# Layer 0's attention in a different order of pairs: the prompt's blocks first, the memory pairs last, and the sample rows' steps up to two pairs earlier

## What is computed

```python
# prompt: causal, and of the keys it may see each query keeps the 128 with the best indexer score
vals, idx = lax.top_k(indexer_scores(iq, ik, iw, qpos, kpos), n_sel)
o = gqa_sparse_attend(q, take(kv, idx), isfinite(vals))     # 12 heads, 4 key/value heads
# memory: every prompt query against 256 memory tokens
p = softmax(einsum('bthd,bmhd->bhtm', mq, mem_k) * scale);  om = einsum('bhtm,bmhd->bthd', p, mem_v)
# sample: each of the 8 tokens against 256 of its 1024 cached keys and itself (paged cache), and its own 256 memory tokens
```

## Time and profile before

| | |
|---|---|
| median of 3 runs | 2230.3 us (2225.42 to 2233.84) |
| the profiled execution | 2222.14 us |
| its span, first to last instruction | 2220.2 us |
| PE busy in the span | 2103.8 us (95%) |
| DVE busy | 1015.3 us (46%) |
| ACT busy | 701.6 us (32%) |
| PE's mean granted clock | 0.973 of full speed |
| layer 0's attention, first scores to PE's turning of the sample rows' outputs | 585.35 to 731.79 us |
| layer 1's attention, first scores to last output | 1676.63 to 1788.4 us |

### The profile page before, as it was taken

One profiled execution on the slowest core, in us unless ns is written; L12 is line 12 of the kernel. 1 busy time (PEld: TensorE's weight loads), 2 busy tenths in 40 slices (PEclk: granted clock), 3 DMA queues, 4 the chain that ended last, 5 costly groups with the idle time before them and its releaser, 6 DMA issues.

```text
span 2220.2 us, 43049 instructions
## 1 busy us (share of the span) xinstructions
PE 2103.8 (95%) x17509; PEld 2003.5 (90%) x17509; DVE 1015.3 (46%) x1463; ACT 701.6 (32%) x869; POOL 336.8 (15%) x301
## 2 busy tenths in 40 slices
PE   6999999989868899999999999999997789999997
PEld 6999999968635899999999999999995579999997
DVE  7433333566895443333354333335533353333334
ACT  5332222431235333322243322224124443321232
POOL 2110011233222111001111100111511121100111
PEclk9999999989979999999999999999999989999998
DMA  6324423322552232332244234224236012223222
GB/s 222 121 91 141 154 92 106 108 64 65 193 167 76 85 138 83 139 124 94 73 140 152 94 109 147 90 98 173 87 110 231 8 60 93 90 86 109 80 74 74
DMA packets 60067, 246.57 MB, mean 111 GB/s; under 512 B 8642, under 2 KB 30538, under 8 KB 42930
## 3 DMA queue, kind: packets, MB, share of 16 engines
q1 hardware_dynamic: 58082, 212.31, 28.5%
q10 hardware_dynamic: 1872, 32.67, 4.0%
HBM read 234.67 MB, written 34.80 MB: 121 GB/s over the span
## 4 chain that ended last, share of the span: by engine, by line
PE 88%; DVE 6%; ACT 2%; issue 2%; SPq 1%; DMA 0%; ACTq 0%; POOL 0%; DVEq 0%; POOLq 0%
PE ps L556 81%; PE ps L768 1%; PE ps L787 1%; DVE tkw L1791 1%; PE ps L747 1%; DVE tk L1788 1%; ACT pbuf L1188 1%; PE ps L755 1%; ACT wh L1049 1%; DVE a_sc L1860 1%; PE ps L947 1%; SPq L397 0%; DVE wl L1329 0%; PE ps L987 0%; DVE pbuf L1555 0%
## 5 line engine op out<-in xcount | busy, mean ns | idle before, releaser
L556 PE MATMUL ps<-xh,wh 128*128 128x260 f32 x3296 | 666.2, 283 | 3.6 <-ACT wh L1049 2.0
L556 PE MATMUL ps<-xh,wl 128*128 128x260 f32 x3296 | 665.2, 283 | 0.0
L556 PE MATMUL ps<-xl,wh 128*128 128x260 f32 x3296 | 664.2, 283 | 0.0
L1329 DVE TENSOR_TENSOR wl<-raw,wh 128x2048 fp32r<-128x2048 f32 x181 | 420.9, 2325 | 321.3 <-ACT wh L1049 321.3
L556 PEld LDWEIGHTS ps<-xh,wh 128*128 128x128 f32 x3296 | 509.6, 189 | 4.1 <-DVE memv L1382 2.2
L556 PEld LDWEIGHTS ps<-xh,wl 128*128 128x128 f32 x3296 | 509.3, 189 | 0.0
L556 PEld LDWEIGHTS ps<-xl,wh 128*128 128x128 f32 x3296 | 507.9, 189 | 0.0
L1049 ACT ACTIVATE wh<-raw 128x2048 fp32r<-128x2048 f32 x181 | 344.9, 1906 | 348.0 <-PE ps L556 297.0
L556 PE MATMUL ps<-acth,wh 128*128 128x260 f32 x1600 | 324.1, 284 | 10.0 <-DVE actl L1878 7.6
L556 PE MATMUL ps<-actl,wh 128*128 128x260 f32 x1600 | 324.4, 284 | 0.0
L556 PE MATMUL ps<-acth,wl 128*128 128x260 f32 x1600 | 323.4, 284 | 0.0
(11 more groups left out here) (264 smaller groups left out, 1612.3 us busy)
## 6 DMA issues: line engine op xcount, KB each, us to landing
raw<-in_w_ffn_in SPq DMA_DIRECT2D x88, 1024.0 KB, 4.9
raw<-in_w_ffn_out SPq DMA_DIRECT2D x32, 768.0 KB, 4.3
raw<-in_w_ffn_out SPq DMA_DIRECT2D x32, 640.0 KB, 3.9
raw<-in_w_in_b SPq DMA_DIRECT2D x10, 1024.0 KB, 5.0
raw<-in_w_in_a SPq DMA_DIRECT2D x9, 1024.0 KB, 4.9
out_state<-in_state ACTq DMA_DIRECT2D x8, 1022.0 KB, 6.8
ring_w<-in_kpool SPq DMA_DIRECT2D x48, 128.0 KB, 2.4
raw<-in_w_mem SPq DMA_DIRECT2D x4, 1024.0 KB, 7.1
```

The source lines that it names most:

```text
L556: mm = pe.matmul(o, w(kt), moving, start=(kt == 0 and i == 0), stop=(kt == nk - 1 and i == 2))
L1329: dve.tensor_tensor(wl[:, n % 2, :], raw[:, n % 2, :], wh[:, n % 2, :].bitcast(F32), ALU.subtract)\
```

## The change

`pairs_a` now returns the 24 prompt pairs first and the 8 memory pairs behind them: block 0 is u 0 to 5, block 1 is 6 to 11, block 2 is 12 to 17, block 3 is 18 to 23, memory is 24 to 31. Pairs below u = 20 share one PSUM room for their scores whatever their width, pairs from 20 on use two. The sample rows' steps from "even" on move forward by one or two pairs on PE ("even" from k = 6 to 5, "odd" from 13 to 11, "turn" from 16 to 14, "turn_new" from 18 to 16) and by two pairs on ACT; on DVE the masking of those scores moves from k = 14 to 12, and the inversions stay at k = 18. `VALUES_AFTER`, the search's four steps in each k, the ring of buffers and SP's order stay as they are. Layer 1 keeps its order and its rooms.

```diff
 def pairs_a():

-    pairs = pairs_mem(6)
+    pairs = []
     for blk in range(NBLK):
         for tile in range(len(PAIRS_A)):
             pairs.append(dict(kind="a", blk=blk, tile=tile, cols=(blk + 1) * P, kv=2 * (tile // 3), out=tile))
-    return pairs
+    return pairs + pairs_mem(6)
...
+        ROWS_UNTIL = 20
         ATTEND_AHEAD = {"mem": 2, "a": 2, "b": 1}
...
-                one = q["cols"] <= 256
+                one = u < ROWS_UNTIL if u < len(pairs[0]) else q["cols"] <= 256
...
-        ROWS_AT = {0: "first", 3: "turn_mem", 6: "even", 13: "odd", 16: "turn", 18: "turn_new"}
+        ROWS_AT = {0: "first", 3: "turn_mem", 5: "even", 11: "odd", 14: "turn", 16: "turn_new"}
         VALUES_AFTER = {20: ("mem", 0), 21: ("mem", 1), 23: ("a", 0), 30: ("a", 1)}
-        FIRST_WIDE = next(q["u"] for q in pairs[0] if q["cols"] > 256 and q["u"] % 2)
+        FIRST_WIDE = ROWS_UNTIL + 1
...
-                elif k == 15:
+                elif k == 13:
                     act.wait_ge(rows_masked, 2)
...
-                elif k == 17:
+                elif k == 15:
                     act.wait_ge(rows_turned, 2)
...
-                elif k == 19:
+                elif k == 17:
                     act.wait_ge(rows_turned, 3)
...
-                elif k == 14:
+                elif k == 12:
                     dve.wait_ge(r_used, items_of("a", "key", 0)[-1]["r"] + 1)
```

## The result

The changed kernel takes 2240.48 us (median of 14 runs, 2232.25 to 2245.69), the kernel before 2233.51 in 14 runs beside it (2225.42 to 2236.24). The ratio is 1.0034, with a 95% interval of 1.0023 to 1.0045: by it 7.6 us slower (5 to 10), less than the 0.5% that was called telling. The forecast had been +8.3 us, within 0.5%.

What follows compares the result with a forecast made beforehand. DVE's search was taken to set the pace until 672, PE after; waits and late value loads moved output turning from 731.79 to 740.1, +8.3 us. Added to 2230.3, this gave 2238.6 us, range 2229 to 2247.

Steps and rivals of the forecast that it cites:

- "odd" begins behind the last key load: Layer 0's attention: moved two pairs earlier, "odd" must wait on PE for the last key load, landing at 638.3.
- pair 18 masked, pair 19's scores begin: End of DVE's search: six remaining search steps and `select` run first; pair 18 masked at 674.0, scores 19 waiting for it.
- first cached values end: PE finishes the weighing after pair 23 at 707.2, where it was 699.05.
- The last value items: SP's unchanged 25.27 us load chain after pair 23 ends at 732.5; PE waits some 11 us instead of 1.75.
- the wait of "odd" for its load: PE reaches "odd" at about 635.6, stands until 638.3; DVE then stands 2.8 us (bounds 1.4 and 5).
- the first term: Start of the attention: the first three maskings and linked work are narrower, gaining 1.9 us by the end of step 1.
- a late "even": "Even" late by a us or two costs nothing, swallowed by the wait at "odd".
- PE from 676.15 to 709.83: PE's work from pair 18 masked to first cached values' end: 31.5 us plus 1.7 for half clock.
- Half clock after the long wait: Last cached values, 4.16 us before, take 1.5 us more after 11 idle us (bounds 0 and 4).
- PE at half clock through block 2: Rival, steps 12 to 15: DVE waits 1.7 us in each; +15 us, 2245.5; chance 0.18.
- The hidden last loads: Rival: the last value loads cause no wait; -4.8 us, 2225.5; chance 0.08.
- a gain: Rival: over 11 us faster, needing DVE's stage to end earlier with more pairs masked; chance 0.02 for the rest.

Runs made afterwards that it cites:

- a_values_early: Changed kernel with the sample rows' values weighed after pairs 17, 18, 19, 30 instead of 20, 21, 23, 30; stretch 145.4 us, ratio 0.9982 to the kernel before.
- b_rows_early: Kernel before, its pair order kept, with only the sample rows' steps moved forward as in the change; stretch 147.9 us, ratio 0.9989 to the kernel before.
- a_numbers_ahead: Changed kernel with SP reading the last three sequences' page numbers earlier, while waiting for a buffer; stretch 149.5 us, ratio 1.0003 to the kernel before.
- mem_between_only: Changed kernel with memory pairs moved between blocks 2 and 3, values and four-step search unchanged; stretch 145.2 us, ratio 1.0004 to the kernel before.
- mem_between: Changed kernel with memory pairs between blocks 2 and 3, values after 17, 18, 19, 30, search spread to k = 19; stretch 132.8 us, ratio 0.9930 to before.
- mem_between_late: Same as mem_between, but values weighed after pairs 20, 21, 23, 30 as in the changed kernel; stretch 147.4 us, ratio 1.0003 to the kernel before.
- a_search_five: Changed kernel with five search steps in each k instead of four; stretch 154.7 us, ratio 1.0035 to the kernel before.
- a_rows_later: Changed kernel with the sample rows' steps from "even" on one k later (6, 12, 15, 17); stretch 156.0 us, ratio 1.0020 to the kernel before.
- b_values_early: Same as b_rows_early, but values weighed after pairs 17, 18, 19, 30; stretch 141.3 us, ratio 0.9993 to the kernel before.

## Why the prediction was right, point by point

With 2.1 us added for the later start of the stretch, the forecast's times stand against the rows above as follows:

| step of the prediction | forecast + 2.1 | measured |
|---|---|---|
| "odd" begins behind the last key load | 640.4 | 640.64 |
| "odd" ends | 645.4 | 645.49 |
| pair 14 masked from | 647.8 | 647.84 |
| pair 18 masked, pair 19's scores begin | 676.1 | 676.15 |
| first cached values end | 709.3 | 709.83 |
| last values begin | 734.6 | 734.94 |
| last values end | 740.3 | 740.93 |
| outputs turned | 742.2 | 743.01 |

**The last value items** decided, as forecast: +8.3 in the sum, +9.1 in the stretch, +7.6 timed. That the values' place in the new order, not the sample rows' moved steps, did it is shown by a_values_early and b_rows_early; that 8.3 of the 25 us are register loads on SP, by a_numbers_ahead. (The prediction's "23 us up to the last landing" are the issuing alone; the last load landed some 2 us behind it.) On the Trainium skill's page "DMA: Bandwidth & Descriptors", section "Issuing engines are not separate DMA queues", the time to initiate a DMA "is usually small relative to the DMA itself". The runs here speak against using that on this chain, for with the same bytes and the register loads out of the way it became 8.3 us shorter.

**The term that came out otherwise** is the wait of "odd" for its load. The prediction let PE come to it 2.7 us early (at 635.6, or 637.7 with the shift) and made DVE stand 2.8 us for that. PE came at 640.26 and waited 0.38, and DVE stood 0.74. The rest had been lost earlier: DVE began step 12 at 646.41, forecast 644.4. More than half of these 2 us stand in the rows: "even" at the new k began behind scores at half clock, took 5.30 us and not 3.64, and DVE waited 0.73 and 0.53 us behind it. Another 0.4 us is the first term: DVE's first store began 15.4 us after the first scores (602.85) where it was 16.9 (602.27), a gain of 1.5 us and not 1.9. The prediction had said that a late "even" would be swallowed by the wait for the load; it was, nearly to the last tenth, and the end of "odd" came out right. So the load decided when "odd" could begin, but in this execution the cost wasn't the load's alone.

How this term divides, and how large it is, changes from one execution to the next. Three other kernels are the same as the changed one up to there. DVE's store behind "odd" in a_values_early:

```profile
648.12 0.29 DVE L1581 COPY tg<-ps 128x128 f32<-128x128 f32 x1 [2.33 <-PE ps L797]
```

and in a_numbers_ahead:

```profile
646.90 0.29 DVE L1584 COPY tg<-ps 128x128 f32<-128x128 f32 x1 [2.13 <-PE ps L800]
```

With the 0.74 or 0.75 at the masking that follows, DVE stood 3.1 and 2.9 us there, close to the forecast's 2.8, and in mem_between_only 0.75, as in the changed kernel. Pair 14 was masked from 62.6, 61.4 and 60.4 us after the first scores; the forecast and the changed kernel have 60.4. So the forecast's size for this wait lies within what the executions show, and that the table agrees to some tenths is in part luck of the execution that was profiled: in another the lines from pair 14 on would lie some 2 us later.

**PE from 676.15 to 709.83** took 33.7 us, forecast 33.2. **Half clock after the long wait**: the last values took 5.99 us (734.94 to 740.93), forecast 5.66 (4.16 and 1.5).

**The rivals.** PE at half clock through block 2 did not occur: from 654 to 668 its weighings took 0.66 us and PE waited for DVE, not DVE for PE, as at 668.02. (It did run at half clock ahead of the rival's place, in the scores at 633.97 and 638.61.) The hidden last loads did not occur either: 10.89 us of idle. Neither did a gain.

**What the prediction did not see** is that idle time at the end of the search and the exposed chain can have one remedy. It took the places of the values as given. In mem_between the values stand beside the end of the search, fill the first and shorten the second. In the changed order itself early values mend only the chain: in a_values_early the wait in front of pair 19's scores is still 6.88 us, for PE comes to the values behind those scores.

## What to carry to other kernels

Work hung into a loop by an index moves in time when the loop's items change order, so for each such index ask two things again: what covers the chain that starts behind it, and what its own work used to cover. A block of work that needs only one engine (the values on PE, `select` on DVE) is worth placing beside a block that needs only the other one; in mem_between that was worth 14.6 us of the stretch (1.7 of them not the edit's), about half of it because PE's clock fell less, where the new order by itself was worth nothing. And a chain of small issues on one queue is priced from its rows, register loads included, not from its bytes.

## What the runs showed of the hardware that was not expected

A short wait can cost more than its length, and the length doesn't say the price. The weighing of the last cached values is the same work in every kernel; this is how long it took behind the wait in front of it:

| kernel | wait, us | last cached values, us | mean granted clock |
|---|---|---|---|
| b_rows_early | 1.19 | 4.15 | 1.00 |
| before | 1.75 | 4.16 | 1.00 |
| mem_between_late | 2.56 | 5.84 | 0.71 |
| a_numbers_ahead | 2.56 | 6.98 | 0.58 |
| mem_between_only | 2.88 | 5.85 | 0.71 |
| a_search_five | 10.18 | 6.93 | 0.58 |
| after | 10.89 | 5.99 | 0.68 |
| a_rows_later | 11.36 | 7.40 | 0.55 |

The price of the wait runs from nothing to 3.2 us, and among the six longer waits it has no order by length: the same 2.56 us cost 1.7 and 2.8. No rule for the length is read from this. Nor does the clock fall only at a wait's end. In b_values_early PE stood 3.91 us, its scores behind that still ran at full clock, and only the transposes after them at half (1.88 us instead of 1.09):

```profile
655.58 0.70 PE L755 MATMUL ps<-tiles 64*128 64x256 f32 x4 [3.91 <-DVE stats L1555]
656.21 1.88 PE L855 MATMUL ps<-ident,work 128*128 128x128 f32 x8
```

In the changed kernel the transposes ahead of a wait of 3.19 us were at half clock already (1.12 us at 629.67, where 0.66 is the time at full), and the scores behind it stayed there (1.65 instead of 0.92). That bursts behind long waits each begin at half rate is what the Trainium skill says ("TensorE: Matmul & The Clock Gate", section "HAM oscillation — how this bites in real kernels"). The rows here agree in kind but not row by row: in mem_between_late and b_values_early the first matmuls behind the wait still ran at full clock.
